# Attention scores from three f32r products instead of one f32 product, in a two-layer trunk on one Trainium2 core

## What is computed

```python
def block(j):
    qj = lax.dynamic_index_in_dim(qb, j, axis=1, keepdims=False)
    kj = lax.dynamic_slice_in_dim(kp, j * A_WINDOW, 2 * A_WINDOW, axis=1)
    vj = lax.dynamic_slice_in_dim(vp, j * A_WINDOW, 2 * A_WINDOW, axis=1)
    s = jnp.einsum('bqkgd,bskd->bkgqs', qj, kj) * scale
    valid = band & (ki + j * A_WINDOW - A_WINDOW >= 0)
    s = jnp.where(valid, s, -jnp.inf)
    sink = jnp.broadcast_to(sink_logits, s.shape[:-1] + (1,))
    p = jax.nn.softmax(jnp.concatenate([s, sink], axis=-1), axis=-1)[..., :-1]
    return jnp.einsum('bkgqs,bskd->bqkgd', p, vj)
...
return (a * jax.nn.silu(z)) @ w_out.astype(F32)
```

## Time and profile before

| | us |
|---|---|
| median of three runs | 3034.83 (3031.55 to 3037.38) |
| the profiled execution, its time | 3025.52 |
| the profiled execution, its span | 3023.7 |
| PE busy | 2765.6 (91%) |
| DVE busy | 1558.9 (52%) |
| ACT busy | 1103.1 (36%) |
| POOL busy | 640.8 (21%) |
| start of the attention stage in the span | 2626.5 |

### The profile page before, as it was taken

The page is one execution under the profiler, slowest core; times in us unless marked ns, Lnnn a source line. Parts: engine busy times, 40 slices in busy tenths (PEclk is TensorE's granted clock), DMA queues, the critical chain, the costliest instruction groups (busy, mean ns, idle before and its releaser), DMA issues. The chain is left out here.

```text
span 3023.7 us, 36865 instructions
## 1 busy us (share of the span) xinstructions
PE 2765.6 (91%) x13163; PEld 2195.2 (73%) x13163; DVE 1558.9 (52%) x3227; ACT 1103.1 (36%) x2442; POOL 640.8 (21%) x526
## 2 busy tenths in 40 slices
PE   4799998999999799689997699997899999899999
PEld 2677887888888678578785577776677777667776
DVE  5565771556655456453223666664534431456664
ACT  2611221222222222334331455553522222366664
POOL 0004661544545100032232000000100000033332
PEclk7899999999999899899998899999899999999999
DMA  7216446454454465698896465662422324512221
GB/s 252 95 67 149 146 145 155 138 149 144 147 157 138 151 218 178 211 251 238 256 276 193 133 178 168 165 171 79 167 73 74 88 76 122 166 60 89 85 85 63
DMA packets 454027, 445.66 MB, mean 147 GB/s; under 512 B 157556, under 2 KB 349388, under 8 KB 450380
## 3 DMA queue, kind: packets, MB, share of 16 engines
q1 hardware_dynamic: 350340, 337.75, 38.0%
q10 hardware_dynamic: 103504, 105.54, 10.8%
HBM read 282.06 MB, written 162.74 MB: 147 GB/s over the span
## 5 line engine op out<-in xcount | busy, mean ns | idle before, releaser
L2771 PE MATMUL a_pg<-a_hT,a_whl 128*128 128x512 f32 x640 | 256.7, 401 | 3.4 <-DVE a_whl L878 3.4
L2772 PE MATMUL a_pg<-a_hT,a_whl 128*128 128x512 f32 x640 | 251.1, 392 | 0.0
L2773 PE MATMUL a_pg<-a_hT,a_whl 128*128 128x512 f32 x640 | 250.9, 392 | 0.0
L884 PE MATMUL p_g<-hT,w_hl 128*128 128x512 f32 x512 | 212.2, 415 | 0.0
L830 PE MATMUL pg<-hT,w_hl 128*128 128x512 f32 x512 | 206.3, 403 | 6.5 <-DVE w_hl L878 6.5
L832 PE MATMUL pg<-hT,w_hl 128*128 128x512 f32 x512 | 201.9, 394 | 0.0
L831 PE MATMUL pg<-hT,w_hl 128*128 128x512 f32 x512 | 201.7, 394 | 0.0
L886 PE MATMUL p_g<-hT,w_hl 128*128 128x512 f32 x512 | 200.2, 391 | 0.0
L885 PE MATMUL p_g<-hT,w_hl 128*128 128x512 f32 x512 | 199.8, 390 | 0.0
L2771 PEld LDWEIGHTS a_pg<-a_hT,a_whl 128*128 128x128 f32 x640 | 121.4, 190 | 42.0 <-DVE a_whl L878 11.4
L2773 PEld LDWEIGHTS a_pg<-a_hT,a_whl 128*128 128x128 f32 x640 | 121.3, 189 | 26.3
(11 more groups left out here) (502 smaller groups left out, 6848.9 us busy)
## 6 DMA issues: line engine op xcount, KB each, us to landing
s_wt<-s5w_d SPq DMA_DIRECT2D x64, 354.0 KB
vo_d<-e_stage ACTq DMA_DIRECT2D x64, 256.5 KB, 8.5
w_raw<-in_ev_w_in SPq DMA_DIRECT2D x32, 512.0 KB, 5.7
s5w_d<-gate_sums SPq DMA_DIRECT2D x32, 512.0 KB, 3.0
shared<-h_d SPq DMA_DIRECT2D x28, 512.0 KB, 4.1
arena<-in_ada_w SPq DMA_DIRECT2D x8, 1536.0 KB, 11.6
e_ada_w<-in_ada_w SPq DMA_DIRECT2D x32, 384.0 KB, 7.4
a_raw<-in_od_w_in SPq DMA_DIRECT2D x40, 256.0 KB, 3.4
```

The lines of the kernel that those rows point to most:

```text
L884: nc.tensor.matmul(out, w(0, k), x(0, k), start=(k == 0), stop=False)
L2771: mm(bank, w[:, 0, k, :], x[:, 0, k, :], start=(k == 0), stop=False)
L2772: mm(bank, w[:, 0, k, :], x[:, 1, k, :], start=False, stop=False)
L2773: last = mm(bank, w[:, 1, k, :], x[:, 0, k, :], start=False, stop=(k == KC - 1))
```

## The change

Keys and queries are split inside the attention stage. ACT rounds them to f32r (`k_hi`, `q_round`) and DVE takes the difference (`k_lo`, `q_part`), which it writes over the original. Keys are split in five pieces, the first (256 columns) ahead of the loop and the others at G = 0 to 3. Queries are split a tile at a time: tile 0 ahead of the loop, tile t+1 at G = 4t+1, on ACT ahead of `y_part`, on DVE behind `maxima`. Each score product is three f32r products that add up in PSUM. PE waits for `q_split` and `k_split` at the first step of a tile. Three small buffers move to make room: the third score buffer lies in `m.gate`, the y buffers behind the rings, the rounded queries in `m.spare`. The diff:

```diff
@@ -177,6 +177,7 @@
     m.ident = ctx.enter_context(nc.sbuf_tensor("ident", [P, P], F32))
     m.cols = ctx.enter_context(nc.sbuf_tensor("cols", [P, P], F32))
     m.ada = ctx.enter_context(nc.sbuf_tensor("ada", [P, 2, 24], F32))
+    m.spare_at = nc.sbuf_base
     m.spare = ctx.enter_context(nc.sbuf_tensor("gate_sums", [P, SEQ], F32))
     m.gacc = m.spare[0:2 * MH]
     m.decay = ctx.enter_context(nc.sbuf_tensor("decay", [P, MH, NMC], F32))
@@ -2845,14 +2846,19 @@
     with ExitStack() as ctx:
         sb = lambda n, s, d=F32: ctx.enter_context(nc.sbuf_tensor(n, s, d))
         kT, vv, mask, first = m.kT, m.vv, m.mask, m.mask0
+        khl = [sb("b_k_hi", [P, 2, P + SEQ], F32R), nc.alloc_sbuf_tensor_at("b_k_lo", [P, 2, P + SEQ], F32R, offset=m.kT_at)]
+        q_hi = [nc.alloc_sbuf_tensor_at(f"b_q_hi{j}", [P, KC, P], F32R, offset=m.spare_at + 4 * j * D) for j in range(2)]
+        q_lo = [nc.alloc_sbuf_tensor_at(f"b_q_lo{j}", [P, KC, P], F32R, offset=m.shared_at + 4 * (m.shared_used + ((j - 1) if j else -2) * D))
+                for j in range(3)]
+        pieces = (0, 2 * P, P + BT, P + 2 * BT, P + 3 * BT, P + 4 * BT)
         rest = m.shared[:, m.shared_used:]
         cut = [rest[:, j * D:(j + 1) * D] for j in range(9)]
         qt = [m.qt0[:]] + [x.rearrange("p (i c) -> p i c", i=KC) for x in cut[0:2]]
         zt = [m.zt0[:]] + [x.rearrange("p (i c) -> p i c", i=KC) for x in cut[2:4]]
         ht = cut[4:7]
-        sc = [x.rearrange("p (h c) -> p h c", h=4) for x in cut[7:9]] + [sb("b_sc", [P, 4, 2 * P])[:]]
+        sc = [x.rearrange("p (h c) -> p h c", h=4) for x in cut[7:9]] + [m.gate[:].rearrange("p (h c) -> p h c", h=4)]
         pT = [sb(f"b_pT{j}", [P, 2, 4, P]) for j in range(2)]
-        yf = [sb(f"b_y{j}", [P, 2, P]) for j in range(2)]
+        yf = [rest[:, 9 * D + 2 * P * j:9 * D + 2 * P * (j + 1)].rearrange("p (r c) -> p r c", r=2) for j in range(2)]
         yhl = [sb(f"b_yhl{j}", [P, 2, KC, P], F32R) for j in range(2)]
         sink = m.sink
         st = [sb(f"b_stat{j}", [P, 5, 4]) for j in range(3)]
@@ -2865,6 +2871,7 @@
         q_in, z_in, h_in, o_out = ([m.sem(f"b_{n}{j}") for j in range(3)] for n in ("q_in", "z_in", "h_in", "o_out"))
         s_done, s_read, max_ready, exp_ready, inv_ready, p_ready, p_turned, pT_ready = S(
             "s_done s_read max_ready exp_ready inv_ready p_ready p_turned pT_ready")
+        k_rounded, k_split, q_rounded, q_split = S("k_rounded k_split q_rounded q_split")
         pv_done, y_ready, y_hi, y_lo, o_done, o_added = S("pv_done y_ready y_hi y_lo o_done o_added")
         dve = Tally(m.sem("b_dve"))
         ring_uses = lambda t: t // 3 + (1 if t % 3 else 0)
@@ -2944,9 +2951,25 @@
                     act.wait_ge(y_ready, G + 1)
                     if t >= 2:
                         act.wait_ge(o_done, 4 * (t - 1))
-                    nc.scalar.copy(yhl[t % 2][:, 0, i:i + 2, :], yf[G % 2][:]).then_inc(y_hi, 1)
-
+                    nc.scalar.copy(yhl[t % 2][:, 0, i:i + 2, :], yf[G % 2]).then_inc(y_hi, 1)
+
+                def k_hi(i):
+                    cols = slice(pieces[i], pieces[i + 1])
+                    nc.scalar.copy(khl[0][:, :, cols], kT[:, :, cols]).then_inc(k_rounded, 1)
+
+                def q_round(t):
+                    act.wait_ge(*((q_in[t % 3], 16 * ring_uses(t)) if t else (m.q_in, 16)))
+                    if t >= 2:
+                        act.wait_ge(s_done, 4 * (t - 1))
+                    nc.scalar.copy(q_hi[t % 2][:], qt[t % 3]).then_inc(q_rounded, 1)
+
+                k_hi(0)
+                q_round(0)
                 for G in range(STEPS + 3):
+                    if G < 4:
+                        k_hi(G + 1)
+                    if G % 4 == 1 and G // 4 + 1 < TT:
+                        q_round(G // 4 + 1)
                     if G >= 3:
                         y_part(G - 3)
                     if 2 <= G < STEPS + 2:
@@ -2993,10 +3016,10 @@
                         v.wait_ge(*((z_in[t % 3], 16 * ring_uses(t)) if t else (m.z_in, 16)))
                     if G >= 2:
                         v.wait_ge(y_lo, G - 1)
-                    tt(yf[G % 2][:], pv[G % 2][:, 0:2 * P].rearrange("p (r c) -> p r c", r=2), zt[t % 3][:, 2 * g:2 * g + 2, :],
+                    tt(yf[G % 2], pv[G % 2][:, 0:2 * P].rearrange("p (r c) -> p r c", r=2), zt[t % 3][:, 2 * g:2 * g + 2, :],
                        ALU.mult).then_inc(y_ready, 1)
                     v.wait_ge(y_hi, G + 1)
-                    tt(yhl[t % 2][:, 1, 2 * g:2 * g + 2, :], yf[G % 2][:], yhl[t % 2][:, 0, 2 * g:2 * g + 2, :].bitcast(F32),
+                    tt(yhl[t % 2][:, 1, 2 * g:2 * g + 2, :], yf[G % 2], yhl[t % 2][:, 0, 2 * g:2 * g + 2, :].bitcast(F32),
                        ALU.subtract).then_inc(y_lo, 1)
 
                 def output(c):
@@ -3007,6 +3030,17 @@
                     cols = ht[t % 3][:, n * 512:(n + 1) * 512]
                     tt(cols, cols, po[n][:], ALU.add).then_inc(o_added, 1)
 
+                def k_lo(i):
+                    v.wait_ge(k_rounded, i + 1)
+                    cols = slice(pieces[i], pieces[i + 1])
+                    tt(khl[1][:, :, cols], kT[:, :, cols], khl[0][:, :, cols].bitcast(F32), ALU.subtract).then_inc(k_split, 1)
+
+                def q_part(t):
+                    v.wait_ge(q_rounded, t + 1)
+                    tt(q_lo[t % 3][:], qt[t % 3], q_hi[t % 2][:].bitcast(F32), ALU.subtract).then_inc(q_split, 1)
+
+                k_lo(0)
+                q_part(0)
                 v.wait_ge(m.sink_in, 16)
                 for G in range(STEPS + 9):
                     if 3 <= G < STEPS + 3:
@@ -3015,6 +3049,10 @@
                         inverse(G - 1)
                     if G < STEPS:
                         maxima(G)
+                    if G < 4:
+                        k_lo(G + 1)
+                    if G % 4 == 1 and G // 4 + 1 < TT:
+                        q_part(G // 4 + 1)
                     if G >= 9 and (G - 8) % 2 == 1 and (G - 8) // 2 < 2 * TT:
                         output((G - 8) // 2)
 
@@ -3026,14 +3064,16 @@
                     t, g = divmod(G, 4)
                     Q, x = heads(g)
                     if g == 0:
-                        pe.wait_ge(*((q_in[t % 3], 16 * ring_uses(t)) if t else (m.q_in, 16)))
+                        pe.wait_ge(q_split, t + 1)
+                        pe.wait_ge(k_split, 1 if t == 0 else t // 4 + 2)
                     if G:
                         pe.wait_ge(s_read, G)
                     for r in range(2):
-                        for h in range(2):
-                            rows = slice(AD * h, AD * (h + 1))
-                            last = mm(psc[:, 2 * h + r, :], qt[t % 3][rows, 4 * Q + 2 * x + r, :], kT[rows, Q, P * t:P * t + 2 * P],
-                                      start=True, stop=True)
+                        for e, (w, k) in enumerate(((q_hi[t % 2], khl[0]), (q_hi[t % 2], khl[1]), (q_lo[t % 3], khl[0]))):
+                            for h in range(2):
+                                rows = slice(AD * h, AD * (h + 1))
+                                last = mm(psc[:, 2 * h + r, :], w[rows, 4 * Q + 2 * x + r, :], k[rows, Q, P * t:P * t + 2 * P],
+                                          start=(e == 0), stop=(e == 2), skip_group_check=True)
                     last.then_inc(s_done, 1)
 
                 def turn(G):
@@ -3128,6 +3168,7 @@
         m.gate = ctx.enter_context(nc.sbuf_tensor("gate_row", [P, D], F32))
         m.mask, m.mask0 = (ctx.enter_context(nc.sbuf_tensor(f"mask{j}", [P, 2 * P], F32)) for j in range(2))
         m.sink = ctx.enter_context(nc.sbuf_tensor("sinks", [P, 2, 2, 2, 2], F32))
+        m.kT_at = nc.sbuf_base
         m.kT = ctx.enter_context(nc.sbuf_tensor("keys", [P, 2, P + SEQ], F32))
         m.shared_at = nc.sbuf_base
         m.shared = ctx.enter_context(nc.sbuf_tensor("shared", [P, NB * part], F32))
```

## The result

| | before | after |
|---|---|---|
| median of six runs each, us | 3033.8 (3031.1 to 3037.7) | 3046.6 (3039.7 to 3050.0) |
| ratio, 95% interval | | 1.0040 (1.0026 to 1.0054) |
| span of the profiled execution | 3023.7 | 3037.9 |
| attention stage | 411.2 | 420.9 |
| twelve middle tiles, M(11) to M(59), each | 23.41 | 24.00 |

The change makes the kernel 0.4% slower, 12.9 us by the medians, with an interval of 8 to 16. P(G) and M(G) are the starts of `scores(G)` and `maxima(G)` as in the prediction. The attention stage is counted from SP's load of the first query tile, 14 us ahead of the first work of `attend`, to the end. It grew by 9.7. The profiled executions differ by 4.5 more ahead of that point (2612.5 against 2617.0), in code that the change doesn't touch.

What follows compares the result with a forecast made beforehand. PE bounds the kernel before; after, a loop over output, store and q load, 23.88 us per tile. Ramp +4.5, twelve such tiles and four PE steps of 5.70 give +7.8 on the 3034.8 median: 3042.6 us, range 3029 to 3050.

Steps and rivals of the forecast that it cites:

- The bound before: Attention stage, steps 7 to 63: PE bounds at 5.855 us each; the DVE/ACT cycle has 0.43 us a step in hand.
- the loop after: Twelve later tiles: output, store, h load, q load, `q_round`, cast, maxima, two more steps; 23.88 us per tile, over PE's 22.80.
- The mean landing: Load of a query tile: q is there 10.95 us after M(4T-5), with 2.7 for the store and 5.0 for the load.
- The rival of unpaired products: Scores on PE: f32r pairs don't run side by side, steps take 6.34 to 6.46, +32 to +38 us; chance 0.10.
- The ramp: Steps ahead of M(7): added rounding and difference copies delay M(7) by +4.5 us in sum, give or take 1.5.
- step 1: Ramp: `k_lo` and `q_part` need 2.4 us in a window of 2.3, so +0.1.
- step 3: Ramp: the last `k_hi` stands between exps and the first cast, +0.96 us.
- step 5: Ramp: `q_round(2)` on ACT costs +0.96 us.
- DVE's window: DVE between M + 2.13 and the cast at M + 4.34: `q_part`, output and product, some 2.1 us, hidden within 0.1.
- The end of the sum: After M(59) PE takes over: scores(60) at + 2.0 us, four steps of 5.70, nothing changed from there; +7.8 in all.
- Rival 1: Twelve tiles: q is there when ACT asks, PE stays the bound, -4.2 us, time 3030.6; chance 0.14.
- point of decision: ACT's wait for q: whether the reload hides is decided by q landing before or after 9.8 us behind M.

Runs made afterwards that it cites:

- q_early: Against the changed kernel, SP issues the load of query tile t+4 ahead of store(t) instead of behind store(t) and h_tile(t+3); ratio 0.9986 to the kernel before.
- q_past_h: Against the changed kernel, SP issues the load of query tile t+4 right behind store(t), ahead of h_tile(t+3); ratio 0.9985 to the kernel before.
- before_q_early: The kernel before, nothing split, with SP's load of query tile t+4 moved ahead of store(t); ratio 0.9991 to the kernel before.
- before_again: The kernel before once more, without edit; one run, 3043.7 us, attention stage 414.0 us.
- after_again: The changed kernel once more, without edit; ratio 1.0041 to the kernel before, attention stage 420.9 us.
- one_product: Against the changed kernel, two of the three score products left out, only rounded by rounded kept in f32r, all copies and waits staying; ratio 1.0029 to the kernel before.

## Why the prediction was right, and where it was off

- The bound before (PE, with DVE and ACT 0.43 us behind) and the loop after were as forecast, with the loop's length 24.00 for 23.88. The mean landing was 11.09 for 10.95: the stores took 2.9 on average, not 2.7. (The prediction's own terms, 2.13 + 0.71 + 2.7 + 0.38 + 5.0, add up to 10.92.) Twelve times 0.12 is 1.4 us of the missing time.
- Scores piece: 0.91 forecast, 0.90 measured; pairs 0.118, measured 0.117. The rival of unpaired products is out. The Trainium skill ("FP8 and Floating Point Precision", TensorE Precision Notes) counts four passes for true FP32; with three of the four for the three products the estimate was 0.85, and this trace does not agree: 0.90. For the time of the kernel neither mattered.
- The ramp: first scores +2.9 (2.9 forecast), M(0) then comes 0.42 sooner (0.4), step 1 +0.0 (0.1), step 3 +0.94, step 5 +0.95 (0.96 each). M(7) is +4.4 for +4.5. What the prediction did not see is that the ramp of before has two forms 2.8 us apart; it took the shorter for the rule, and of the three profiles without the change two have the longer. Here it was lucky: in after the rise came 34.4 us after the start of the stage, as in the longer form (34.5; 26.7 in the shorter), and nothing in the prediction said that this would cost the changed kernel nothing.
- `q_part` was to fit in DVE's window within 0.1 and did: the step behind each rounding is 5.42.
- The end of the sum: `scores(60)` was put at M(59) + 2.0. It came at + 2.6, for PE, not DVE, was last there by then. That step was mis-sized by 0.6.
- Sum: +7.8 forecast, +9.7 in the stage of the profiled pair, +12.9 by the medians. The 1.9 between the first two are the 1.4 and 0.6 above, less 0.1 in the ramp. The rest, 3.2, lies ahead of the stage or in the choice of executions; against the longer form of the ramp of before the stage grew by 6.9, and the rest is 6.0. So the mechanism is shown, and 3.2 to 6.0 of the 12.9 have no cause shown here. The start of the stage scattered from 2612.5 to 2627.9 over three profiles without the change and from 2617.0 to 2633.0 over ten with it. On one and the same chip it came at 2618.4 without the change and at 2618.4, 2620.5 and 2628.8 with it, on another at 2627.9 without and at 2623.4 and 2633.0 with it, so no direction is seen. It goes along, roughly, with TensorE's clock ahead of the stage, which was granted at 0.50 for 238.9 us in the profile with the earliest start and for 266.2 us in the one with the latest; why it differs is open. The interval of the ratio (8 to 16 us) holds 9.7, but not 6.9. No run separates a small effect ahead of the stage from chance.
- Rival 1 (the reload hides, 3030.6, a ratio of 0.9986) did not happen, but it is what q_early measured, 0.9986: its price was right to within what the ramp's two forms leave open (the stage came out 3.9 or 6.7 under that of before, for 4.2), and its point of decision, q at M + 9.8, was bracketed by q_past_h (8.1, no wait) and after (11.1).

## What to carry to other kernels

When a copy is put ahead of a use, it moves the time at which its input is wanted: look up where in the queue that load stands and what it stands behind, and add up the way from the last instruction it waits for. An output, its store, the landing and a load made a way of 11 us in a loop of 24 that no busy time shows. Then ask what stands behind the new wait on its engine; one place further down in ACT's order the same wait cost nothing. The Trainium skill says to issue a DMA early and wait late ("DMA: Bandwidth & Descriptors", Rules for kernel authors); by this trace, the change had moved the waiting three steps forward and left the issue where it was.

## What the runs showed of the hardware

- f32r matmuls of 64 rows and 256 columns run side by side on the two row halves, a pair every 0.117 us at a granted clock of 2.4 GHz, with a weight load of 128 columns for each (steps 38 and 39 of after).
- The rise of TensorE's clock in the ramp came at 12.7 us after the first scores in one execution of the kernel before and at 20.3 and 20.4 in two others (one of them before_q_early), with PE's last work ahead of the stage 3.6 us before the first scores in all three, and moved the end by 2.8 us. One profile against another can mislead by that much. Stages in which the rise came at the same place repeated to 0.1 us (before_again and before_q_early, after and after_again).
- Store landings of 512 KB have a tail: median 2.6, up to 3.8 in after and 4.5 in one_product; with the load of q issued right behind them (q_past_h) median 3.1, up to 5.1. In a loop, the mean counts.
